# Two-block language model forward pass: chunks of 4, 6, 6 and 6 tiles in the feed-forward layers, weight rounding ahead of the gate's activation, and another order of GpSimd's rests

## The reference

```python
def swiglu(h, w_gate, w_up, w_down):
    return (jax.nn.silu(h @ w_gate) * (h @ w_up)) @ w_down
...
x = x + 0.5 * swiglu(rms_norm(x, ffn1_norm[i]), ffn1_w_gate[i], ffn1_w_up[i], ffn1_w_down[i])
x = x + hybrid_mixer(...)
x = x + 0.5 * swiglu(rms_norm(x, ffn2_norm[i]), ffn2_w_gate[i], ffn2_w_up[i], ffn2_w_down[i])
...
h = h + gdn_mixer(...)                                          # second block, i = 0
h = h + swiglu_2(rms_norm_2(h, ln_ffn[i]), ffn_w_in[i], ffn_w_out[i])
h = h + (p[i] @ ple_w_proj[i]) * jax.nn.sigmoid(rms_norm_2(h, ln_ple[i]) @ ple_w_gate[i])
h = h + sb_mixer(...)                                           # i = 1, then the same two again
```

## Time and profile before

| | us |
|---|---|
| median of 3 runs | 2540.82 |
| lowest and highest | 2537.53, 2541.53 |
| time of the profiled execution | 2540.85 |
| its span, from the first to the last instruction | 2539.1 |

### The profile page before, as it was taken

One profiled execution on the slowest core, in us unless ns is written; L12 is line 12 of the kernel. 1 busy time (PEld: TensorE's weight loads), 2 busy tenths in 40 slices (PEclk: granted clock), 3 DMA queues, 4 the chain that ended last, 5 costly groups with the idle time before them and its releaser, 6 DMA issues.

```text
span 2539.1 us, 34828 instructions
## 1 busy us (share of the span) xinstructions
PE 2483.5 (98%) x14086; PEld 2078.0 (82%) x14086; DVE 1430.4 (56%) x2049; ACT 1181.2 (47%) x1737; POOL 1230.0 (48%) x610
## 2 busy tenths in 40 slices
PE   8999999999999999999999999999999999999999
PEld 6888887777788898777878788898877767898887
DVE  6444352878573443586766663443587567443345
ACT  5232243568453333567455642332555685332333
POOL 3664644222446555456544355655444124655644
PEclk9999999999999999999999999999999999999999
DMA  4332333121323323222111123333332112333323
GB/s 140 108 98 86 117 102 114 58 67 50 100 76 107 100 91 106 86 83 85 50 35 35 51 94 107 100 100 94 98 93 86 47 42 91 109 100 96 104 92 124
DMA packets 61774, 223.43 MB, mean 88 GB/s; under 512 B 6704, under 2 KB 6832, under 8 KB 61488
## 3 DMA queue, kind: packets, MB, share of 16 engines
q1 hardware_dynamic: 60928, 218.07, 27.3%
q10 hardware_dynamic: 688, 3.15, 0.4%
HBM read 219.10 MB, written 2.10 MB: 87 GB/s over the span
## 4 chain that ended last, share of the span: by engine, by line
PE 75%; DVE 11%; ACT 7%; issue 3%; POOL 2%; DMA 1%; SPq 0%; DVEq 0%; ACTq 0%; POOLq 0%
PE ps L424 7%; PE ps L426 7%; PE ps L425 7%; PE ps L587 5%; PE ps L588 5%; PE ps L589 5%; PE ps L536 3%; PE ps L537 3%; PE ps L538 3%; PE ps L528 2%; PE ps L527 2%; PE ps L526 2%; PE ps L913 2%; PE ps L915 2%; PE ps L914 2%
## 5 line engine op out<-in xcount | busy, mean ns | idle before, releaser
L2885 POOL TENSOR_TENSOR w_lo<-raw,w_hi 128x1024 fp32r<-128x1024 f32 (+1 forms) x405 | 960.7, 2380 | 1167.2 <-ACT w_hi L445 1167.0
L445 ACT ACTIVATE w_hi<-raw 128x1024 fp32r<-128x1024 f32 (+1 forms) x405 | 409.4, 1013 | 486.9 <-PE ps L426 265.3
L587 PE MATMUL ps<-x_hi,w_hi 128*128 128x512 f32 x784 | 308.5, 393 | 10.2 <-DVE x_lo L483 8.1
L588 PE MATMUL ps<-x_lo,w_hi 128*128 128x512 f32 x784 | 305.8, 390 | 0.0
L589 PE MATMUL ps<-x_hi,w_lo 128*128 128x512 f32 x784 | 305.3, 389 | 0.0
L425 PE MATMUL ps<-mid_lo,w_hi 128*128 128x512 f32 x736 | 286.5, 389 | 0.0
L424 PE MATMUL ps<-mid_hi,w_hi 128*128 128x512 f32 x736 | 286.5, 389 | 0.0
L426 PE MATMUL ps<-mid_hi,w_lo 128*128 128x512 f32 x736 | 286.5, 389 | 0.0
L819 DVE SCALAR_TENSOR_TENSOR h<-ps,h 128x512 f32<-128x512 f32 x128 | 87.5, 690 | 265.2 <-PE ps L426 265.2
L645 ACT ACTIVATE ff_gate<-ff_gate 128x512 f32<-128x512 f32 x88 | 55.4, 630 | 374.8 <-DVE ff_gate L770 322.6
L2892 POOL TENSOR_TENSOR t_lo<-t_sum,t_hi 128x1024 fp32r<-128x1024 f32 x78 | 191.8, 2481 | 10.8 <-ACT t_hi L450 10.8
(11 more groups left out here) (449 smaller groups left out, 5777.8 us busy)
## 6 DMA issues: line engine op xcount, KB each, us to landing
raw<-in_units_dram SPq DMA_DIRECT2D x406, 512.0 KB, 3.5
h<-in_x_t_dram SPq DMA_DIRECT2D x4, 512.0 KB, 6.4
toep<-in_rel_table_dram ACTq DMA_DIRECT2D x1, 2048.0 KB, 7.7
out_dram<-h SPq DMA_DIRECT2D x4, 512.0 KB, 5.5
p_f<-in_p_t_dram ACTq DMA_DIRECT2D x2, 512.0 KB, 4.4
const<-in_constants_dram SPq DMA_DIRECT2D x1, 832.0 KB, 6.6
vec<-in_vectors_dram SPq DMA_DIRECT2D x1, 137.5 KB, 2.2
```

The lines of the kernel that those rows point to most:

```text
L445: nc.scalar.activation(w_hi[:, n % W_SLOTS, begin:], raw[:, n % RAW_SLOTS, begin:], ACT.Copy).then_inc(s_whi, 1)
L587: nc.tensor.matmul(out, hi, x_hi[:, k, :], start=(k == 0), stop=False)
L588: nc.tensor.matmul(out, hi, x_lo[:, k, :], start=False, stop=False)
L2885: nc.gpsimd.tensor_tensor(w_lo[:, n % W_SLOTS, begin:], raw[:, n % RAW_SLOTS, begin:], w_hi[:, n % W_SLOTS, begin:].bitcast(F32), ALU.subt ...
```

## The change

1. The chunks are 4, 6, 6, 6 tiles. Strassen tiles: FFN 0 none in its first chunk and (0, 2, 4) in the other three, FFN 1 to 3 tile 3 in the first chunk and (0, 2, 4) in the others. There were 9, 10, 10 and 10 Strassen tiles and there still are.
2. ScalarE rounds unit 2t+4 ahead of the silu of tile t, unless tile t+1 is a Strassen tile.
3. GpSimd makes `t_lo` part 0, then the up unit's `w_lo`, then `t_lo` part 1.
4. At the start of FFN 1 to 3 ScalarE rounds unit 3 before the scaled copies of the input, and units 4 and 5 before it rounds the input sums.
5. In FFN 0 VectorE makes part 0 of the input sums after tile 1 and part 1 after tile 2 (before: both after tile 1), and ScalarE rounds them after tile 3 (before: after tile 2).
6. The two tiles of `p` for the embedding go to slots 6 and 7 of `mid_hi` and `mid_lo`.

```diff
-HALVES = (6, 6, 6, 4)
-STRASSEN = (((5,), (0, 2, 4), (0, 2, 4), (0, 2)),) + (((3, 5), (0, 2, 4), (0, 2, 4), (0, 2)),) * 3
+HALVES = (4, 6, 6, 6)
+STRASSEN = (((),) + ((0, 2, 4),) * 3,) + (((3,),) + ((0, 2, 4),) * 3,) * 3
...
         def act_ffn(act, w, eps, own, gain, load_p=None, late=False):
-            if not late:
-                act_x_parts(act, w, own)
...
                         act_rstd(act, w, 4 * (g ^ 1), eps)
+                        act_ahead(act, n0, 0, 2)
                     else:
+                        act_ahead(act, n0, 0, 0)
+                        act_x_parts(act, w, own)
                         act_rstd(act, w, 4 * (g ^ 1), eps)
-                        act_ahead(act, n0, 0, 0)
                         act_ahead(act, n0, 0, 1)
+                        act_ahead(act, n0, 0, 2)
                         act_x_sum(act, w, 0)
                         act_x_sum(act, w, 1)
-                    act_ahead(act, n0, 0, 2)
...
                 for t in range(tiles):
                     pair = t % 2
+                    early = t + 1 not in picked
                     if 2 * t >= ahead:
                         act_ahead(act, n0, 0, 2 * t)
+                    if 2 * t + 1 >= ahead and early:
+                        act_ahead(act, n0, 0, 2 * t + 1)
                     act.wait_ge(s_free, b0 + 2 * t + 5)
                     nc.scalar.activation(ff_gate[:, pair, :], ff_gate[:, pair, :], ACT.Silu).then_inc(s_act1, 1)
-                    if 2 * t + 1 >= ahead:
+                    if 2 * t + 1 >= ahead and not early:
                         act_ahead(act, n0, 0, 2 * t + 1)
...
-                    if half == 0 and late and t == 2:
+                    if half == 0 and late and t == 3:
                         act_x_sum(act, w, 0)
                         act_x_sum(act, w, 1)
...
-                        if half == 0 and late and t == 1:
-                            dve_x_sums(dve, w, own, 0)
-                            dve_x_sums(dve, w, own, 1)
-                        if half == 0 and late and t == 2:
+                        if half == 0 and late and 1 <= t < 3:
+                            dve_x_sums(dve, w, own, t - 1)
+                        if half == 0 and late and t == 3:
                             dve_x_sums_lo(dve, w, 0)
                             dve_x_sums_lo(dve, w, 1)
-                        if half == 0 and t == picked[0] - 2:
+                        if half == 0 and picked and t == picked[0] - 2:
...
-                for n in range(pool_at[0], end):
-                    begin = T if n - 1 in S_GATES else 0
+                def weight_lo(n, begin):
                     pool.wait_ge(s_whi, n + 1)
                     nc.gpsimd.tensor_tensor(w_lo[:, n % W_SLOTS, begin:], raw[:, n % RAW_SLOTS, begin:], w_hi[:, n % W_SLOTS, begin:].bitcast(F32),
                                             ALU.subtract).then_inc(s_wlo, 1)
-                    if begin:
-                        x = S_OF[n]
-                        for part in range(2):
-                            pool.wait_ge(s_tsum, 4 * x + 4)
-                            pool.wait_ge(s_thi, 2 * x + part + 1)
-                            nc.gpsimd.tensor_tensor(t_lo[x % 2][part][:, :, :], t_sum[x % 2][part][:, :, :],
-                                                    t_hi[x % 2][:, 2 * part:2 * part + 2, :].bitcast(F32), ALU.subtract).then_inc(s_tlo, 1)
+
+                def sums_lo(x, part):
+                    pool.wait_ge(s_tsum, 4 * x + 4)
+                    pool.wait_ge(s_thi, 2 * x + part + 1)
+                    nc.gpsimd.tensor_tensor(t_lo[x % 2][part][:, :, :], t_sum[x % 2][part][:, :, :],
+                                            t_hi[x % 2][:, 2 * part:2 * part + 2, :].bitcast(F32), ALU.subtract).then_inc(s_tlo, 1)
+
+                for n in range(pool_at[0], end):
+                    if n - 1 in S_GATES:
+                        sums_lo(S_OF[n], 0)
+                        weight_lo(n, T)
+                        sums_lo(S_OF[n], 1)
+                    else:
+                        weight_lo(n, 0)
                 pool_at[0] = end
             def ffn_walk():
```

More of the change, by code:

```diff
@@ L160 @@
 S_GATES = strassen_units()
+FIRST_OF = [sum(len(p) for layers in STRASSEN[:f] for p in layers) for f in range(4)]
 S_OF = {n + side: x for x, n in enumerate(S_GATES) for side in range(2)}
@@ L575, in pe_ffn @@
                         pe_strassen(pe, w, S_OF[n0 + 2 * t], n0 + 2 * t, b0 + 2 * t + 1, b0 + (2 * t + 3 if t == tiles - 1 else max(2 * t + 2, 4)),
-                                    g, t % 2, up_bank(g, t, tiles), half == 0 and t == picked[0])
+                                    g, t % 2, up_bank(g, t, tiles), S_OF[n0 + 2 * t] == FIRST_OF[w.ffn])
                         continue
@@ L658, in act_ffn @@
                     for k in range(2):
-                        nc.scalar.activation(mid_hi[:, 4 + k, :], p_f[:, k, :], ACT.Copy).then_inc(s_phi, 1)
+                        nc.scalar.activation(mid_hi[:, 6 + k, :], p_f[:, k, :], ACT.Copy).then_inc(s_phi, 1)
                 w.mids += tiles
@@ L803, in dve_ffn @@
                     for k in range(2):
-                        nc.vector.tensor_tensor(mid_lo[:, 4 + k, :], p_f[:, k, :], mid_hi[:, 4 + k, :].bitcast(F32), ALU.subtract).then_inc(s_plo, 1)
+                        nc.vector.tensor_tensor(mid_lo[:, 6 + k, :], p_f[:, k, :], mid_hi[:, 6 + k, :].bitcast(F32), ALU.subtract).then_inc(s_plo, 1)
                 w.mids += tiles
@@ L2349, in pe_embed @@
                 plo = w.plo
-                pe_square_half(pe, w, 2, lambda k: (mid_hi[:, 4 + k, :], mid_lo[:, 4 + k, :]), lambda k: pe.wait_ge(s_plo, plo + k + 1))
+                pe_square_half(pe, w, 2, lambda k: (mid_hi[:, 6 + k, :], mid_lo[:, 6 + k, :]), lambda k: pe.wait_ge(s_plo, plo + k + 1))
             w.plo += 2
```

## The result

The changed kernel takes 2548.26 us (median of 6 runs, 2544.18 to 2550.78). The kernel before takes 2540.34 in the same comparison (6 runs, 2537.53 to 2541.53). The ratio is 1.0027, with a 95% interval of 1.0016 to 1.0039: the change makes the kernel **slower by 0.27%**, 7 to 8 us. (This ratio and the later ones are estimates over all the runs compared. They need not equal the quotient of the two medians, which is 1.0031 here.) The forecast was 10.7 us faster, 2530.1, with a range of 2521 to 2537. It was wrong. The profiled execution took 2548.59 us.

A forecast was written before the change was run, and what follows sets the result against it. TensorE, busy 98% of the 2539.1 us span, was taken as the bound, with 21.3 us of waits to win. Gains 6.15 + 1.2 + 3.7 - 0.4 = 10.7 took 2540.85 to 2530.1 us, range 2521 to 2537.

The forecast's parts named there:

- Tile 5 of the first chunks: Second Strassen tiles of the four feed-forward layers' first chunks disappear, saving 4.93 us in FFN 0 and 6.15 in FFN 1 to 3.
- GpSimd's new order: Third Strassen tiles of chunks 2 to 4: `t_lo` part 1 ends as before; 0.1 us lost in each of 12, 0.4 more in all.
- The sign that I had named: If the third Strassen tiles of chunks take over 11 us, GpSimd's order is wrong and the time is above 2535.
- the pair that takes turns: VectorE and GpSimd share a port pair and work one at a time; each due rest costs VectorE up to 2.4 us.
- the new order hurts the thirds: Rival, 5%: at worst 1.15 us and a 0.26 restart in each of 12 third Strassen tiles, 17 us; 2547.
- The 0.15 us of margin: In a chunk's third Strassen tile, `t_lo` part 1 ends at 165.17 and is needed at 165.3, so no wait.
- FFN 0, first chunk: TensorE waits 3.3 us for `mid_lo`, 4.8 with a clock fall, then 0.7 and 0.8; loss 6.3 against 7.5, gain 1.2.
- FFN 1 to 3, tile 3: First chunks: waits before the fourth product, losing 0.9 in FFN 1 and 1.5 each in FFN 2 and 3; gain 3.7.
- The rest: Copies of `p`, the moved `act_x_parts` (3.3 us) and the longer last chunk cost nothing.

The follow-up runs named there:

- the kernel with one wait more: Changed kernel, but GpSimd makes the gate unit's rest of each later chunk's second and third Strassen tile only after that tile's four weight sums; 2530.48 us, ratio 0.9957.

## Why the prediction was wrong

**Tile 5 of the first chunks** (4.93 in FFN 0, 6.15 in the others): right. The tiles are gone and their losses with them.

**The failing step is "GpSimd's new order".** It took the moment at which `t_hi` is ready, 158.6, from the profile of before and let everything run from there. Under this premise the working holds: in the kernel before with item 3 alone the 8 thirds lose 1.1 us together, and in the changed kernel without item 2 the 12 thirds lose 3.0. The premise failed because item 2 moves `t_hi`. I had costed item 2 only in the first chunks. In the chunks 2 to 4 it rounds the gate unit of the next Strassen tile before the silu of a Strassen tile. Its rest then begins 8.6 us into the first Strassen tile (193.76 - 185.16) and not 12.9 (131.92 - 119.06), and so it falls on the weight sums. The term was some 0.1 us of loss in each of 12 thirds, 0.4 more than before in all; it measured 20.0, which is 19.1 more than before. The step is off by 18.7, more than the whole forecast gain. Not all of this is the collision. With it taken away (the kernel with one wait more) the thirds still lose 3.3, and 2.1 of that is the third of FFN 0's second chunk, which is late from the first chunk on; the pair of items costs the other 16.7. The sign that I had named came true as well: the shortest third took 11.15 us, and the time is above 2535.

I had the mechanism in hand. The paragraph on the pair that takes turns says that each rest that is due costs VectorE up to 2.4 us, and it read long instructions in the first chunks. The rule stated by the Trainium skill (SBUF — State Buffer, "Who interferes with whom"), one of the two blocked fully, is what the sum of 2.90 us shows: it is 2.2 longer than the 0.69 that it takes alone, and it ends 0.55 behind the rest (196.72 against 196.17). I asked where rests **are** due beside VectorE's long rows, and not where the change **puts** a rest that wasn't there. The thirds that I had followed were those of the kernel before.

**The rival "the new order hurts the thirds"** gave 2547 at 5%, and 2548 came. Its price was near: 1.41 in each of 12 thirds, 17 in all, where the thirds lost 19.1 more than before. That the total came so near is in part luck: besides the 2.1 more that the thirds lost, the rest of the feed-forward layers won 1.3 more than it assumed (12.4 against 11.1). Its place was right too, part 1: all 12 thirds wait 0.8 or 0.9 us there, and six of them wait at part 0 as well, up to 1.56. Its condition was the wrong way round. I wrote that it decides if the next gate's rest does **not** come forward, and held against it that the raw slot is filled in time. The rest did come forward, and that did the harm: GpSimd had it behind itself and still sat idle until `t_hi` (6.46 and 7.67 us in the lines above). The 0.15 us of margin that I had worked out for part 1 should have been the warning: a term that rests on 0.15 us in 12 places, with two edits that touch its inputs, has both ends open.

**FFN 0, first chunk.** The form was right: no wait for `w_lo` any more and a wait for `mid_lo` in the down projection, at 67.8, where 69.3 was forecast. Its size was 1.7 in place of 3.3:

```profile
67.81 0.50 PE L425 MATMUL ps<-mid_hi,w_hi 128*128 128x512 f32 x1 [1.68 <-DVE mid_lo L745]
```

The turns came as forecast. In part 0 of the input sums two instructions of VectorE, one behind the other, each took the time of one of GpSimd's two rests, and the next took 0.47 again:

```profile
46.81 2.67 DVE L701 SCALAR_TENSOR_TENSOR sx_sum<-h,vec,x_part 128x256 f32<-128x256 f32 x1
49.41 2.61 DVE L699 SCALAR_TENSOR_TENSOR sx_sum<-h,vec,x_part 128x256 f32<-128x256 f32 x1
```

```profile
46.80 4.93 POOL L2887 TENSOR_TENSOR w_lo<-raw,w_hi 128x1024 fp32r<-128x1024 f32 x2 [2.24 <-ACT w_hi L446]
```

But each of the four parts of VectorE's row (sums, tile 2, sums, tile 3) was 0.1 to 0.7 shorter than I had it, 1.5 in all. The granted clock stayed at 1.00 from 57.80 to 82.52. Up to the end of the second chunk's first Strassen tile 4.5 us were lost, and I had 6.3. The prediction has no term for lateness that lasts: the second Strassen tile loses another 2.5 (1.6 without item 2), and the third 3.0 (2.2 without item 2).

**FFN 1 to 3, tile 3.** Forecast a loss of 3.9, measured 1.5, so 2.4 better than forecast. The wait is before the fourth product in FFN 2 and 3, as said. Without item 2 it is 3.3, and with item 2 in the first chunks alone 1.55.

**The rest** (`p`, the moved copies, the longer last chunk) costs nothing in the feed-forward layers that a row shows.

In sum: the first chunks, with the Strassen tile behind that of FFN 0, came out 4.2 us better than forecast, the second Strassen tiles of all chunks 2.9 worse (2.5 of it in FFN 0's second chunk), and the thirds 18.7 worse: -10.7 - 4.2 + 2.9 + 18.7 = 6.7. The span grew by 7.7. The last 1.0 lies between the last Strassen tile of FFN 1 and the first of FFN 2, where the matmuls of a mixer run; I did not follow it.

## What to carry to other kernels

Two edits that are each harmless can take the same slack: here one made an input 2.1 us late and the other gave away the filler work that would have hidden it. When a step is made earlier, look at what runs **at its new time** on engines that share something with it, in every stage in which it moves and not only in the one that it is meant for; and when a margin is a few tenths, forecast it for the changed kernel's inputs, not for those of before. An extra wait that keeps two engines off each other can be worth more than the earliness that it gives up.

## What the runs showed of the hardware

A GpSimd rest of 2.4 us that starts 0.06 us ahead of a VectorE weight sum of 0.69 makes that sum 2.90 long. The next one took 0.69 again, and no further rest was due until long after. In the run with the old order of the rests the two started together at 190.38. There the sum at 190.38 went through in 0.69 and the next took 2.77, and the rest was 2.95 long in place of 2.40. In the changed kernel's nine tiles it is the same: the third sum was the long one where the rest led it by 0.06 us or more (four tiles), and the fourth where the rest began between 0.02 ahead of the third and 0.10 behind it (five tiles). So some hundredths decide which instruction is stretched, but the row of sums is 2.1 to 2.2 us longer each time.

With several rests due in a row, the lines at 46.81 and 49.41 show one VectorE instruction stretched for each of them.

No wait for `t_lo` in the changed kernel, the longest of 1.56 us, took the granted clock below 1.00 over its tile, and neither did the 1.68 for `mid_lo`. Between 1.7 and 2.0 us both outcomes are in the runs. Over the tile with the wait, the clock was 0.87 or 0.88 after 1.75 (items 2 and 3 undone, 125.61 to 139.17), 1.80 (item 2 alone in the kernel before, 759.30 to 772.92), 1.86 and 2.01 (the kernel before, FFN 1's tile 5 and FFN 3's tile 3 in the earlier trace rows). It was 1.00 after 1.75 and 1.82 (item 2 alone in the kernel before, 1511.00 to 1523.08 and 2176.96 to 2189.10) and after 2.00 (FFN 2's tile 3). A fall costs some 1.5 us: busy time 11.8 in place of 10.3. The length of a wait alone does not tell which it will be.
